# A two-block transformer kernel: the scan's triangular inverse on 32x32 diagonal blocks, Gram products between its levels, and gate columns moved behind the scan

## The reference, cut to what matters

```python
def step(state, inp):
    r_t, w_t, k_t, v_t, kk_t, a_t = inp
    sa = jnp.einsum('bhvk,bhk->bhv', state, -kk_t)
    state = (state * w_t[:, :, None, :]
             + sa[..., None] * (kk_t * a_t)[:, :, None, :]
             + v_t[..., None] * k_t[:, :, None, :])
    y_t = jnp.einsum('bhvk,bhk->bhv', state, r_t)
    return state, y_t
...
mean = jnp.mean(y, axis=-1, keepdims=True)
var = jnp.mean(jnp.square(y - mean), axis=-1, keepdims=True)
y = ((y - mean) * lax.rsqrt(var + GN_EPS)).reshape(b, s, D_A) * ln_g + ln_b
return (y + bonus.reshape(b, s, D_A)) * gate
```

## Time and profile before

| | |
|---|---|
| median of 3 runs | 3445.56 us |
| profiled execution | 3436.36 us |
| its span, first to last instruction | 3434.5 us |
| TensorE busy | 3151.6 us (92%) |
| VectorE busy | 1494.9 us (44%) |
| ScalarE busy | 802.7 us (23%) |
| GpSimd busy | 636.4 us (19%) |
| mean granted TensorE clock | 0.946 |

### The profile page before, as it was taken

How to read it: one execution, slowest core, us unless ns; L and a number is a source line. 1 busy time by engine, 2 the same in 40 slices (tenths; PEclk the granted TensorE clock), 3 DMA queues, 4 the chain that set the end, 5 groups by cost and what they waited for, 6 DMA issues and landing times. The chain is left out here.

```text
span 3434.5 us, 51714 instructions
## 1 busy us (share of the span) xinstructions
PE 3151.6 (92%) x22119; PEld 2147.9 (63%) x22119; DVE 1494.9 (44%) x2451; ACT 802.7 (23%) x1128; POOL 636.4 (19%) x580
## 2 busy tenths in 40 slices
PE   7988999999788889999994999988999999988999
PEld 3765334433256553334442998787798898787798
DVE  2334333323353243233325556673454655773454
ACT  1211111111013011111111335422233434522232
POOL 3511233333155022333332000020000000020000
PEclk9978999999888889999997999899999999999999
DMA  8635999999966369999997543202454553202452
GB/s 296 239 114 216 407 376 395 385 383 377 371 224 232 142 254 402 380 379 385 380 383 287 198 170 117 74 27 93 154 184 159 192 174 139 74 27 88 156 188 86
DMA packets 305358, 799.19 MB, mean 233 GB/s; under 512 B 57038, under 2 KB 155876, under 8 KB 251244
## 3 DMA queue, kind: packets, MB, share of 16 engines
q1 hardware_dynamic: 245804, 727.16, 56.3%
q0 software_dynamic: 58784, 66.64, 5.9%
q10 hardware_dynamic: 544, 2.10, 0.2%
HBM read 988.60 MB, written 53.48 MB: 303 GB/s over the span
## 5 line engine op out<-in xcount | busy, mean ns | idle before, releaser
L808 PE MATMUL f_bank<-f_ringA,f_arena 128*64 128x512 f32 x3072 | 688.0, 601 | 14.8 <-DMA f_ringA<-in_w_up,f_chosen 10.4
L808 PEld LDWEIGHTS f_bank<-f_ringA,f_arena 128*64 128x64 f32 x3072 | 218.3, 138 | 404.4 <-issue 403.3
L2133 PE MATMUL s_bank<-s_hT_parts,s_highA_parts 128*128 128x256 f32 x1344 | 380.7, 283 | 0.0
L2133 PE MATMUL s_bank<-s_hT_high_parts,s_ringA_parts 128*128 128x256 f32 x1344 | 380.6, 283 | 0.0
L2133 PE MATMUL s_bank<-s_hT_high_parts,s_highA_parts 128*128 128x256 f32 x1344 | 380.6, 283 | 0.0
L829 PE MATMUL f_bank<-f_ringB,f_arena 128*64 128x512 f32 x1536 | 346.3, 592 | 2.1 <-DVE f_arena L1595 2.1
L1580 DVE TENSOR_TENSOR f_arena<-f_arena,f_bank 128x256 f32<-128x256 f32 x96 | 58.7, 612 | 594.0 <-ACT f_arena L1190 594.0
L1111 ACT ACTIVATE f_arena<-f_bank 128x512 f32<-128x512 f32 (+1 forms) x266 | 144.8, 583 | 605.6 <-PE f_bank L789 323.3
L2133 PEld LDWEIGHTS s_bank<-s_hT_high_parts,s_highA_parts 128*128 128x128 f32 x1344 | 258.2, 192 | 1.4
L2133 PEld LDWEIGHTS s_bank<-s_hT_parts,s_highA_parts 128*128 128x128 f32 x1344 | 258.1, 192 | 1.4
L2133 PEld LDWEIGHTS s_bank<-s_hT_high_parts,s_ringA_parts 128*128 128x128 f32 x1344 | 258.1, 192 | 0.0
(11 more groups left out here) (416 smaller groups left out, 5145.7 us busy)
## 6 DMA issues: line engine op xcount, KB each, us to landing
f_ringA<-in_w_gate SPq DMA_DIRECT2D x128, 1024.0 KB
f_ringA<-in_w_up SPq DMA_DIRECT2D x128, 1024.0 KB
f_ringB<-in_w_down SPq DMA_DIRECT2D x128, 1024.0 KB
s_ringA<-in_ffn_in SPq DMA_DIRECT2D x88, 1024.0 KB, 7.7
f_ringA<-in_w_ada SPq DMA_DIRECT2D x46, 1024.0 KB, 13.4
s_arena<-in_ffn_out SPq DMA_DIRECT2D x44, 1024.0 KB, 6.5
s_ringA<-in_w_in SPq DMA_DIRECT2D x40, 1024.0 KB, 6.2
f_ringA<-in_w_in SPq DMA_DIRECT2D x28, 1024.0 KB, 14.0
```

The lines of the kernel that those rows point to most:

```text
L808: last = mm(ps[j * CAP:(j + 1) * CAP, :].rearrange("p (h c) -> p h c", h=2), picked[:, b % 2, k, j * CAP:(j + 1) * CAP], gu[j][:, :, k, :] ...
L2133: last = mm(ps[:, t * S:(t + 1) * S], parts_of(wx[:, k, cs_]), parts_of(hx[:, k, :]), start=(k == 0 and x == 0), stop=(k == DT - 1 and x = ...
```

## The change: the inverse

The triangle is inverted on its two 32x32 diagonal blocks only (SUB = 32), in four levels. X and XT of a group now lie in one array (XX[d][:, q, x]), and one product `quarters` (32 matrix products of 32x32) handles four blocks down the partitions. The L Gram product is gone as such: `small_gram` forms, for both directions and both of X and XT, only the 32x32 diagonal blocks. A fifth level is made off the diagonal: `last_level_left`, `inverse_whole` (which spreads the diagonal blocks into the 64x64 form by a product with the identity) and `last_level_right`. The starting X and XT move from GpSimd to VectorE, the masks Z of each level from VectorE to GpSimd. The full UR and KR products stand between the levels' parts, one half (name, d, q, hh) at a time.

```diff
-        LEVELS = 5
+        LEVELS = 4
+        fillers = [(name, d, q, hh) for name in ("UR", "KR") for d in range(2) for q in range(2) for hh in range(2)]
...
+                def small_gram(q):
+                    ps = [banks.claim(pe, ("LU", q, hh)) for hh in range(2)]
+                    for d in range(2):
+                        for x in range(2):
+                            for a in range(2):
+                                for c in range(NCH):
+                                    for r in range(2):
+                                        s = slice(c * CH + r * SUB, c * CH + (r + 1) * SUB)
+                                        o = c % 2 * CH + r * SUB
+                                        n = 8 * d + 4 * x + 2 * a + c // 2
+                                        for hh in range(2):
+                                            h = slice(hh * HD, hh * HD + HD)
+                                            sides = AR[d][h, 2 * q + a, 0, s], Bt[d][h, 2 * q + a, s]
+                                            last = mm(ps[hh][o:o + SUB, n * SUB:(n + 1) * SUB], sides[x], sides[1 - x],
...
+                def quarters(ps, at, left, right):
+                    for u in range(8):
+                        for o in range(0, P, SUB):
+                            last = mm(ps[o:o + SUB, (at + u) * SUB:(at + u + 1) * SUB], left[o:o + SUB, u],
+                                      right[o:o + SUB, u], start=True, stop=True)
+                    return last
...
+                filler = iter(fillers)
+                for lv in range(LEVELS):
+                    for q in range(2):
+                        pe.wait_ge(z_ready, 2 * lv + q + 1)
...
+                        ps = banks.claim(pe, ("W", q, lv))
+                        for d in range(2):
+                            last = quarters(ps, 8 * d, Z[:, q, d], XX[d][:, q, 0])
+                        banks.fill(last, ("W", q, lv))
+                        gram(*next(filler))
+                    for q in range(2):
+                        banks.evacuated(pe, ("W", q, lv))
+                        for d in range(2):
+                            i = 2 * d + q
+                            ps = banks.claim(pe, ("D", i, lv))
+                            quarters(ps, 0, XX[d][:, q, 1], W1[:, q, d])
+                            banks.fill(quarters(ps, 8, W1[:, q, d], XX[d][:, q, 1]), ("D", i, lv))
+                        gram(*next(filler))
```

Two of the four gate pieces in the scan's steps move behind the scan, so that four stand there. The norm of y loses one VectorE operation, and two large ones (the bonus times the values, plus the norm's offset) are done ahead of the scan. The branch tiles are computed in two runs of four, each run first with `w_branch[0]`, then with `w_branch[1]`, so that the second weight is waited for later:

```diff
-                    half_gates(2 * GATES_EARLY + n)
+                    if n < 2:
+                        half_gates(2 * GATES_EARLY + n)
...
-                half_gates(14)
-                half_gates(15)
+                for i in range(12, 16):
+                    half_gates(i)
...
-                landed(a_wa)
-                landed(a_wb)
...
-                for t in range(DT):
-                    ps = banks.claim(pe, ("branch", t))
+                for first in (0, 4):
                     for half, (n, src) in enumerate(((a_wa, oaT), (a_wb, obT))):
+                        landed(n)
                         w = slotA(n).rearrange("p (k c) -> p k c", k=4)
-                        for k in range(4):
...
+                        for t in range(first, first + 4):
+                            ps = banks.t[banks.uses[("branch", t)][0]] if half else banks.claim(pe, ("branch", t))
+                            for k in range(4):
...
+                step(tt(yadd.rearrange("p (h d) -> p h d", d=HD), Vtok.rearrange("p m (h d) -> p (m h) d", d=HD),
+                        spread(small[:, 240:256], 2, HD), ALU.mult))
+                step(tt(yv, yv, spread(lnx[:, 1, :], 1, MT), ALU.add))
...
-                step(ts(small[:, 120:136], small[:, 120:136], 1.0 / HD, None, ALU.mult))
-                step(tt(t1, yh, spread(small[:, 120:136], 2, HD), ALU.subtract))
+                step(stt(t1, spread(small[:, 120:136], 2, HD), -1.0 / HD, yh, ALU.mult, ALU.add))
...
-                step(tt(ym, ym, spread(lnx[:, 1, :], 1, MT), ALU.add))
-                step(tt(t2, Vtok.rearrange("p m (h d) -> p (m h) d", d=HD), spread(small[:, 240:256], 2, HD),
-                        ALU.mult))
-                step(tt(ytmp, ytmp, ytmp2, ALU.add))
+                step(tt(ytmp, ytmp, yadd, ALU.add))
```

More of the change, by code:

```diff
@@ L1667, in second_block @@
         masks = sb("masks", [P, 13, CH])
+        SUB = CH // 2
         dist = sb("dist", [P, MT, S])
@@ L1881, in plan @@
             for g in range(GATES_EARLY, 8):
-                banks.take(("gates", g), 7)
+                banks.take(("gates", g), 7 if g < 7 else 6)
             for m in range(MT):
@@ L2320, in tensor @@
                 score(1)
-                pe.wait_ge(kk_scaled, 1)
-                for g in range(2):
-                    ps = banks.claim(pe, ("kkb", g))
-                    for t in range(2):
-                        last = mm(ps[:, t * S:(t + 1) * S], headselT[:, 2 * g + t, :], kk_norm, start=True, stop=True)
-                    banks.fill(last, ("kkb", g))
                 score(2)
@@ L2334, in tensor @@
                 half_gates(0)
+                pe.wait_ge(kk_scaled, 1)
+                for g in range(2):
+                    ps = banks.claim(pe, ("kkb", g))
+                    for t in range(2):
+                        last = mm(ps[:, t * S:(t + 1) * S], headselT[:, 2 * g + t, :], kk_norm, start=True, stop=True)
+                    banks.fill(last, ("kkb", g))
                 score(3)
@@ L2395, in own_blocks @@
                     return last
-                tokens_first(0)
+                half_gates(6)
+                turn_comb(2)
+                half_gates(7)
+                values(2)
                 pe.wait_ge(bonus_ready, 2)
@@ L2405, in tensor @@
                 banks.fill(last, "bonus")
-                gram(0, 0)
-                gram(0, 1)
+                tokens_first(0)
+                half_gates(8)
+                pe.wait_ge(ABKR_ready, 2)
+                for q in range(2):
+                    small_gram(q)
+                turn_comb(3)
+                half_gates(9)
+                values(3)
                 tokens_first(1)
-                gram(1, 0)
-                pe.wait_ge(ob_ready, 1)
-                to_features(("obT",), ob, 2)
@@ new lines, in scalar @@
+                take("bonus", bonus, lambda ps: ps[:, 0:16].rearrange("p (m h) -> p m h", m=MT))
+                tokens_first(0)
+                for q in range(2):
+                    for hh in range(2):
+                        ps = banks.read(act, ("LU", q, hh))[:, :].rearrange("p (d x n t) -> p d x n t", d=2, x=2, n=4)
+                        f(Uc[:, q, :, 4 * hh:4 * hh + 4, :], ps[:, :, 1], ACT.Copy).then_inc(u_ready, 1)
+                combined(3)
+                take_gates(4, ACT.Copy)
@@ new lines, in vector, with masked @@
+                obh = ob2.rearrange("p (h d) -> p h d", d=2 * HD)
+                def masked(name, d, q, hh):
+                    out = UM[d] if name == "UR" else KM[d]
+                    key = (name, d, q, hh)
+                    ps = banks.read(dve, key)[:, :].rearrange("p (n r t) -> p n r t", n=4, r=2)
+                    banks.free(tt(out[:, q, 4 * hh:4 * hh + 4], ps, spread(masks[:, d:d + 3:2, :], 1, 4), ALU.mult), key)
+                banks.evacuated(dve, "bonus")
+                filler = iter(fillers)
```

465 lines of the change are left out of this document (269 added, 196 removed).

## The result

| | median us | runs | ratio to before, 95% |
|---|---|---|---|
| before | 3441.56 | 4 (3436.99 to 3446.21) | |
| changed | 3502.77 | 4 (3497.8 to 3505.51) | 1.0176 [1.0155, 1.0198] |

What follows compares the result with a forecast made beforehand. TensorE, busy 92% of the span, was taken as the bound. Per layer 9.8 us won before the scan, 2.4 lost in front, 9.0 won behind: 16.4, both layers 33, giving 3410 us (8 in 10: 3387 to 3448).

Steps and rivals of the forecast that it cites:

- front, to the end of `values(2)`: Mixer's front: the 4.15 us key-norm wait goes, but idle time at `turn_comb(0)` and a low clock follow; 2.4 us lost.
- `small_gram`, 512 records: Diagonal-block Gram products before the levels: 256 products, 512 records at 10 ns each, 5.1 us per layer.
- four levels: The inverse's levels: 768 small records 7.7 us, four Gram halves 3.6, shape changes 1.2; 12.5 us each, 50 for four.
- behind the levels, to the scan's start: From the last level to the scan: old work 13.5 us, plus off-diagonal halves, inverse_whole, turning over, shape changes and waits; 24 us.
- scan and behind it: Two gate pieces move behind the scan and cover the 8.45 us wait for y's norm; 9.0 us won per layer.
- the array is what limits all three, not the issue: Price of a small product: array time sets the cost in all three runs read; 10 ns taken per 32x32 record.
- The prediction's own sign, 128 `quarters` records in 1.0 to 1.3 us: Timeline check in the changed kernel: such a run takes 1.0 to 1.3 us; 1.9 would mean rival 1, 3.4 rival 3.
- corner arithmetic: Record prices per array corner: 58, 108 and 61 ns in three runs, so 50 ns per 64 columns more and 8 beside.
- Rival 1: An issue floor near 14.5 ns a record: levels of 16 us instead of 12.5, no change, 3447 us; chance 0.12.
- Rival 2: The clock falls to half in the 32-wide levels: 21 us a level against 12.5, 3493 us; chance 0.08.
- Rival 3: Records of different tiles do not overlap at 32 columns: 27 ns a small record, 3543 us; chance 0.04.
- Rival 4: The levels wait for other engines at each copy: 2.5 us a level, 20 us in all, 3430 us; chance 0.06.

Runs made afterwards that it cites:

- e3_tail: The kernel before, with only the gate pieces behind the scan, y's addend made ahead of it and the branch products by weight; 3417.19 us against 3437.21.
- e1_wide: The changed kernel with as many records, but seven of eight small products stream 64 columns instead of 32; 3504.99 us, ratio to before 1.0195.
- e4_probe: The kernel before, with stretches of independent small products, long products ahead of each, put in between the gate pieces and the turning over of y; one run, 3667.31 us.
- e6_gates_in: The changed kernel with four gate pieces moved into the levels, one whole piece in each; 3514.58 us, ratio to before 1.0218.
- e8_spread: e6_gates_in with the same four gate pieces issued one product at a time, behind each 64 small records; 3496.81 us, ratio to before 1.0183.

## Why the prediction was wrong

By its steps, for layer 0, in us:

| step | predicted | measured |
|---|---|---|
| front, to the end of `values(2)` | 2.4 lost | 2.8 lost (2237.5 against 2234.7) |
| bonus sums and `tokens_first` | 9.3 | 10.1 |
| `small_gram`, 512 records | 5.1 | 12.2 |
| waits for `combine(3)` and the banks | 3.0 | 0.4 |
| four levels | 50 | 97.9 |
| behind the levels, to the scan's start | 24 | 21.3 |
| sum | 91.4 | 141.9 |
| scan and behind it | 9.0 won | 8.4 won, to the first branch product |

The sum leaves out the work that stands in both kernels, as the prediction's did. Against 101.2 before it is 40.7 lost; with the front and the end, 35 us a layer, 70 in two layers, and the spans differ by 69.2.

- **The step that failed** is the sentence "the array is what limits all three, not the issue", in the price of a small product; the supply of instructions was put at nothing. The array's price was right: 128 records of 32x32 take 1.29 us, the last one's own 0.19 off, 8.7 ns each at full clock, where 8 to 10 were reckoned. But it was read from runs of 32 records, a quarter of a block, which find their instructions ready. A level has 832 records in a row. There the supply gives one each 29.4 ns, and the array's 8.7 ns (13.7 at half clock) are hidden behind that. So a level took 24.5 us where 12.5 were reckoned. The prediction's own sign, 128 `quarters` records in 1.0 to 1.3 us, came true in the first run (1.29), and did not tell: it spans one block, and the cost lies between blocks. Of the miss of 102 us (33 won against 69.2 lost), the levels and `small_gram` are 2 x (47.9 + 7.1) = 110; what went better than reckoned gives some of it back.
- The corner arithmetic hid this, since two limits lay on one number. A two-corner run of 64 columns costs 30 ns by the array, as short runs show (16 records in 0.68 us), and 29.4 ns by the supply. The price of 61 ns a corner fitted the first, so the second was never asked for. For the levels of before, the reading of the array as the limit may well be right, since their run shows no wait for issue (e3_tail's has two, of 0.24 and 0.17 us); it did not carry over to smaller products.
- **The front** went as forecast, 2.8 us lost for 2.4: a wait of 6.32 us before `turn_comb(0)`, then a score pair in 2.07 us and a gate piece in 5.54, at half clock.
- **Behind the levels** the small runs are 64 records between longer ones, and cost what was forecast: 0.75 us for 64 at full clock, 1.07 in two of the four, at half clock.
- **Behind the scan** each point held: the wait is 0.83 us, four pieces take 14.08, `w_branch` is hidden. e3_tail is this step alone: 18 us forecast, 20 between the medians, 15 between the profiled executions.
- **The rivals.** Rival 1 named an issue floor, but priced it at 14.5 ns, the shortest distance in a short run. Rival 2's sign was there, a clock of 0.57, but by e1_wide it costs 3 us a layer there at most, where the rival had 34: TensorE's idle time came first (the clock is 1.00 from 2250 to 2252 and 0.50 from 2254 to 2256, behind the first wait for issue, which ends at 2253.26). Rival 3 had 27 ns a record and 3543 us, nearest to the price, by a mechanism that did not happen: the records do overlap. Rival 4 did not happen; no wait in the levels is for another engine. No rival named the supply, and the range of 3387 to 3448 ended 55 us short.

These are the two windows that the sentence on the clock rests on:

```profile
2250.00:2252.00 2.00, 1.19 (x142) 1.07 (x129) 0.00 (x0) 0.00 (x0) 0.00 (x0) 1.00 0.03 8
...
2254.00:2256.00 2.00, 0.84 (x75) 0.71 (x60) 1.25 (x4) 0.66 (x2) 0.88 (x1) 0.50 0.05 8
```

What would have shown it ahead: TensorE's records in the levels of before, 128 of them at 30.4 ns, are 3.9 us, and the instruction queue brought 12 packets in 50 us there, one each 4 us or so. The two periods stand side by side in the trace of before; neither was read. They would have shown how near the supply was, but not that it can't go faster: for that it takes a run of smaller products, as in e4_probe.

## What to carry to other kernels

Count instructions as well as columns. A long run of short matmuls on TensorE can't go faster than its instructions come, here 256 each 3.76 us on average (3.5 to 4.0), or 29 ns for a matmul and its weight load; below that, a smaller tile is worth nothing unless there are also fewer of them, and a price read from a run shorter than 128 records says nothing of it. Where such a run can't be avoided, mix longer products in one by one, not in a piece, since about one block is made ready ahead. And a wait whose releaser is called "issue" is one for instructions only if the instruction queue brought a packet just ahead of its end; otherwise look for the engine whose work ended there.

## What the runs showed of the hardware that was not expected

- Instructions come to TensorE in 16 KB packets, one each 3.5 to 4.0 us where it waits for them: 4.0 and 3.75 us at half clock, 3.5 at full clock in e4_probe, 3.75 at full clock in e1_wide. After long work 164 to 254 small records run before the first wait: what is left of one block, and the next.
- Why a block takes 3.5 to 4.0 us to come is not shown: the packet itself takes 0.9 to 1.5 us, and TensorE goes on 1.2 to 1.6 us behind its end.
- A small record that finds its instruction ready costs 8.7 ns from start to start (32x32 in four tiles, full clock), and 1.93 us for 128, 13.7 ns, at half clock.
- The granted clock fell from 1.00 to 0.50 behind a wait for instructions of 2.07 us in the changed kernel's `small_gram`. In the levels of e1_wide's layer 0, with twice the columns in each small product and waits of up to 1.86 us, it was 0.96 on average.
- Where large loads ran while small records waited for a block, that one wait was longer than the usual 2 us: 5.1 and 4.5 us in the two layers of e6_gates_in and 4.6 and 4.3 in those of e8_spread (2.1 MB of `w_branch`), 3.8 and 3.3 in e4_probe, where loads were just ending. That the load delayed the packet is likely, but was not tested by itself.
